# A hybrid decoder step: k, q and scratch laid out by pieces of 128 rows, the third pair's strides reordered, and a longer wait ahead of the out stage

## The reference

```python
DIL_CONFIGS = ((128, 1), (512, 4), (2048, 16))     # window, stride d
def _fold(a, d):                                   # tokens r, r+d, r+2d, ... become one sequence
    n, l, h, dh = a.shape
    return a.reshape(n, l // d, d, h, dh).transpose(0, 2, 1, 3, 4).reshape(n * d, l // d, h, dh)
def _dilated_prompt(q, k, v, slopes):
    for window, d in DIL_CONFIGS:
        o, lse = _band_attention(_fold(q, d)[:, :, :, None], _fold(k, d), _fold(v, d), slopes[:, None], d)
        ...
    return _mix_dilations(outs, lses)              # softmax over the three lse
# _band_attention: blocks of 128 rows; row i reads rows i-128..i, bias -slope*d*distance
```

## Time and profile before

| | |
|---|---|
| median of 3 runs | 1440.73 us (1437.33 to 1441.70) |
| profiled execution | 1441.03 us, span 1439.4 us |
| granted PE clock, mean over the span | 0.976 |
| PE / DVE / ACT / POOL busy | 1347.3 / 714.3 / 461.0 / 215.5 us |
| projection, last matmul | about 788.5 us |
| attention | 792.9 to 1179.4 us |
| first matmul of the out stage | 1192.65 us |

### The profile page before, as it was taken

How to read it: one execution, slowest core, us unless ns; L and a number is a source line. 1 busy time by engine, 2 the same in 40 slices (tenths; PEclk the granted TensorE clock), 3 DMA queues, 4 the chain that set the end, 5 groups by cost and what they waited for, 6 DMA issues and landing times.

```text
span 1439.4 us, 21367 instructions
## 1 busy us (share of the span) xinstructions
PE 1347.3 (94%) x7749; PEld 1167.2 (81%) x7749; DVE 714.3 (50%) x1835; ACT 461.0 (32%) x1189; POOL 215.5 (15%) x264
## 2 busy tenths in 40 slices
PE   5869999999999999999999899999889988999896
PEld 2369999999999999999999676777667647877784
DVE  3592122100335454222121658866789447888783
ACT  5440000121111011222111465666558532343431
POOL 0060000000121211000000053125104310111111
PEclk9989999999999999999999899999999998999998
DMA  8524122121353534444335999945935364555531
GB/s 305 210 87 146 44 87 75 56 87 44 117 184 125 176 103 142 131 140 153 98 117 148 247 261 236 219 105 133 231 87 160 99 208 131 158 177 167 164 125 45
DMA packets 132886, 206.23 MB, mean 143 GB/s; under 512 B 13155, under 2 KB 84484, under 8 KB 130605
## 3 DMA queue, kind: packets, MB, share of 16 engines
q1 hardware_dynamic: 119654, 160.12, 37.7%
q0 software_dynamic: 13152, 45.09, 9.7%
HBM read 136.34 MB, written 68.96 MB: 143 GB/s over the span
## 4 chain that ended last, share of the span: by engine, by line
PE 68%; issue 14%; DVE 7%; DMA 5%; ACT 3%; POOL 2%; SPq 2%; POOLq 0%; DVEq 0%; ACTq 0%
PE psum L973 15%; PE psum L974 15%; PE psum L975 15%; PE psum L1079 4%; PE psum L1106 4%; PE psum L1080 3%; PE psum L1090 3%; PE psum L944 2%; DMA dil_v_p<-kv_nat 2%; PE psum L1115 2%; DMA dec_k<-dil_kc 1%; POOL resid L920 1%; DVE h_f L1470 1%; PE psum L1148 1%; DVE logits L1730 1%
## 5 line engine op out<-in xcount | busy, mean ns | idle before, releaser
L973 PE MATMUL psum<-h_hi,w_hi 128*128 128x416 f32 (+1 forms) x1200 | 422.4, 352 | 12.6 <-POOL h_lo L838 12.6
L974 PE MATMUL psum<-h_lo,w_hi 128*128 128x416 f32 (+1 forms) x1200 | 420.2, 350 | 0.0
L975 PE MATMUL psum<-h_hi,w_lo 128*128 128x416 f32 (+1 forms) x1200 | 419.0, 349 | 0.0
L973 PEld LDWEIGHTS psum<-h_hi,w_hi 128*128 128x128 f32 x1200 | 226.2, 188 | 17.9 <-issue 14.8
L974 PEld LDWEIGHTS psum<-h_lo,w_hi 128*128 128x128 f32 x1200 | 226.2, 189 | 1.4
L975 PEld LDWEIGHTS psum<-h_hi,w_lo 128*128 128x128 f32 x1200 | 226.0, 188 | 1.3
L1352 ACT ACTIVATE probs<-logits,stats 128x256 f32<-128x256 f32 (+1 forms) x352 | 162.2, 462 | 150.2 <-DVE stats L1730 143.9
L1730 DVE CUSTOM_DVE_ANT_0 logits<-psum,bias_dil 128x256 f32<-128x256 f32 (+1 forms) x288 | 93.7, 362 | 83.6 <-PE psum L1080 73.2
L973 PE MATMUL psum<-wo_hi,y_hi 128*128 128x512 f32 x288 | 116.9, 406 | 11.0 <-DVE y_lo L1799 10.8
L975 PE MATMUL psum<-wo_hi,y_lo 128*128 128x512 f32 x288 | 114.3, 397 | 0.0
L974 PE MATMUL psum<-wo_lo,y_hi 128*128 128x512 f32 x288 | 113.9, 396 | 0.0
(11 more groups left out here) (249 smaller groups left out, 1769.0 us busy)
## 6 DMA issues: line engine op xcount, KB each, us to landing
w_raw<-w_tiles POOLq DMA_DIRECT2D x30, 512.0 KB, 6.7
k_both<-qk_dram SPq DMA_DIRECT2D x24, 512.0 KB, 12.5
q_both<-qk_dram SPq DMA_DIRECT2D x40, 256.0 KB, 9.7
mix_dram<-o_st POOLq DMA_DIRECT2D x36, 264.0 KB, 6.0
mix_in<-mix_dram SPq DMA_DIRECT2D x16, 594.0 KB, 4.0
gate_dram<-main SPq DMA_DIRECT2D x9, 1024.0 KB, 3.9
qk_dram<-main_hi SPq DMA_DIRECT2D x9, 1024.0 KB, 4.3
qk_dram<-main_lo SPq DMA_DIRECT2D x9, 1024.0 KB, 7.7
```

What stands on the lines that cost most here:

```text
L973: pe.matmul(out, hi, mhi, start=start, stop=False)
L974: pe.matmul(out, hi, mlo, start=False, stop=False)
L975: return pe.matmul(out, lo, mhi, start=False, stop=stop)
```

## The change

Scratch for keys and queries is split. `q_dram` holds for each piece and head a contiguous stack of high rows and low rows; `k_dram` holds every key row twice (index x). One load of 128 rows now fills both halves of `q_both` or `k_both`, where two loads of 64 rows did it before. In exchange, a key tile is stored by eight transfers of 64 rows (each of the two heads' parts written twice, for high and low), a query tile by four of 64 rows; before, both took two transfers of 128 rows.

Keys stand in the scratch and in `k_both` permuted within each block of 128 tokens: first the 32 tokens with number 0 modulo 4, then those with 1, and so on. Keys of stride 4 are then runs of 32 contiguous columns; keys of stride 16 lie 4 columns apart, and a d16 unit reads its own 128 only. The permutation is made when a key tile leaves PSUM (`key_parts`, 11 pieces a tile on ACT and DVE instead of 5). The bias tables of stride 1 and of the window, and the rows of v for these, follow the same permutation; v rows are loaded by four transfers of 32 rows.

The decode and tail rows' transposes and copies move from ahead of attention into its steps 2 to 14, and the first bias tables move ahead, into the evacuation of the last projection tile. The first window load moves ahead of the decode stores on SP. The third pair's phases become d1, d4, d16. The wait before the out stage's first loads is for all 44 group stores.

```diff
-        qk_dram = scratch("qk_dram", [9, 4, 2, 2, 64, 512])
+        q_dram = scratch("q_dram", [5, 4, 2, 2, 64, 512])
+        k_dram = scratch("k_dram", [4, 4, 2, 2, 2, 64, 512])
...
-            for half in range(2):
-                rows = slice(64 * half, 64 * half + 64)
-                eng.dma_start(q_both[kind][rows, :, cols].bitcast(F32),
-                              qk_dram[qt, j, half].rearrange("h r t -> r h t")).then_inc(done, 16)
-                eng.dma_start(k_both[kind][rows, :, cols].bitcast(F32), k.rearrange("a h r t -> r (a h) t")).then_inc(done, 16)
+            k = k_dram[3, j, p:p + 1] if kind else k_dram[p, j]
+            eng.dma_start(q_both[kind][:, :, cols].bitcast(F32),
+                          q_dram[p + 3 * kind, j].rearrange("h a r t -> (a r) h t")).then_inc(done, 16)
+            eng.dma_start(k_both[kind][:, :, cols].bitcast(F32), k.rearrange("h a x r t -> (x r) (h a) t")).then_inc(done, 16)
+
+        def load_v(eng, dst, v, done):
+
+            for r in range(4):
+                eng.dma_start(dst[32 * r:32 * r + 32], v.rearrange("(b j r) c -> r j b c", j=32, r=4)[r]).then_inc(done, 16)
...
+                t = k_both[self.kind][:, part if self.kind else 2 * h + part, 0:T]
                 if self.d == 16:
-                    r0 = self.r - self.r % 2
-                    return v[:, r0:r0 + 2, :]
-                c0 = P * (self.b - 1) if self.full else 0
-                return v[:, self.r, c0:c0 + 256]
+                    return t.rearrange("p (x s i a) -> p s a x i", x=16, s=4, a=4)[:, self.r % 4, self.r // 4]
+                b0 = self.b - 1 if self.full else 0
+                if self.d == 4:
+                    return t.rearrange("p (x s i) -> p s x i", x=16, s=4)[:, self.r, 4 * b0:4 * b0 + 8]
+                return t[:, P * b0:P * b0 + 256]
...
-                  (0, 2, 0), (0, 2, 2), (0, 2, 1))
+                  (0, 2, 0), (0, 2, 1), (0, 2, 2))
...
+        NEW_STEPS = (5, 7, 9, 11, 13)
...
-                        sp.dma_start(qk_dram[t - K0, :, a].rearrange("j h r t -> (h r) j t"),
-                                     part[b][:, 0:T].bitcast(F32).rearrange("p (j t) -> p j t", j=4)).then_inc(done[b], 16)
+                        for h in range(2):
+                            src = part[b][64 * h:64 * h + 64, 0:T].bitcast(F32).rearrange("r (j t) -> r j t", j=4)
+                            if kind == "q":
+                                dst = (q_dram[t - Q0, :, h, a],)
+                            else:
+                                dst = (k_dram[t - K0, :, h, a, x] for x in range(2))
+                            for d in dst:
+                                sp.dma_start(d.rearrange("j r t -> r j t"), src).then_inc(done[b], 16)
...
-                sp.wait_ge(mix_stored[b], 16 * (20 + (b == 0) + 1))
+                sp.wait_ge(mix_stored[b], 16 * (UNITS // 8 + 1))
...
-                    out = psum[:, S_BANK + n % 2, 256 * h:256 * h + 256]
+                    out = psum[:, S_BANK + n % 2, 256 * h:256 * h + (P if u.d == 16 else 256)]
...
-                    pe.wait_ge(zs_copied, 6)
+                    pe.wait_ge(bank_free[4], NT)
...
+                        for a, z in key_parts(c0, c0 + n):
+                            m = nc.scalar.activation(in_keys(main_hi[b], a, z), in_tokens(bank(g), a - c0, z - c0), ACT.Copy,
+                                                     scale=1.0)
...
+                    if ts == NT - 1 and g == 3:
+                        opening()
```

More of the change, by code:

```diff
@@ L413, in main_stores, with lo_stores @@
         def main_stores(ts):
-            return sum(0 if V0 <= t < K0 else 1 for t in range(ts % 2, ts, 2))
+            return sum(0 if V0 <= t < K0 else 4 if K0 <= t < Q0 else 2 if t >= Q0 else 1 for t in range(ts % 2, ts, 2))
+        def lo_stores(ts):
+            return sum(4 if t < Q0 else 2 for t in range(ts % 2, ts, 2) if t >= K0)
         CHUNK0 = 12
@@ L476, in __init__ @@
                 self.full = self.b > 0
-                self.own = P if self.full or (d == 16 and self.r % 2) else 0
-            def view(self, t):
-                return t[:, 0:T].rearrange("p (t r) -> p r t", r=self.d)
+                self.own = P if self.full else 0
             def spread(self, t):
@@ L1155, in _ @@
                 decode(s - LAST)
+                new_rows(s)
                 if s < UNITS:
@@ L1523, in chunk, with pair_tables, opening @@
                 last.then_inc(yac_ready, 1)
+            def pair_tables(i, kind):
+                off = consts[:, C_OFF:C_OFF + 256]
+                by_key = lambda z: z.rearrange("p (x i s) -> p x s i", x=2, s=4)
+                blocks = lambda z: z.rearrange("p (x s i) -> p x s i", x=2, s=4)
+                for h in range(2):
+                    if kind and h == 0:
+                        dve.wait_ge(lo_stored[1], 16 * lo_stores(NT + 1))
+                    if kind == 0:
+                        slope = consts[:, bass.ds(C_SLD + 2 * i + h, 1)]
+                        for c, d in enumerate(DILATIONS):
+                            src, dst = (by_key(off), blocks(bias_dil[:, c, h, :])) if d == 1 else (off, bias_dil[:, c, h, :])
+                            last = dve.tensor_scalar(dst, src, slope, float(d), ALU.mult, ALU.mult)
+                    else:
+                        slope = consts[:, bass.ds(C_SLS + 2 * i + h, 1)]
+                        last = dve.tensor_scalar(blocks(bias_swa[:, h, :]), by_key(off), slope, None, ALU.mult)
+                if kind:
+                    last = dve.tensor_copy(sink_now[:], neg_sink[:, bass.ds(2 * i, 2)])
+                last.then_inc(bias_ready, 1)
+                dve.wait_ge(bias_ready, 2 * i + kind + 1)
+            def opening():
+                dve.wait_ge(lo_stored[0], 16 * lo_stores(NT))
+                dve.wait_ge(kv_t, len(TURNS))
+                dve.tensor_scalar(neg_sink[:], neg_sink[:], -1.0, None, ALU.mult).then_inc(sink_negated, 1)
+                dve.wait_ge(sink_negated, 1)
+                pair_tables(0, 0)
             def gate_rows():
@@ L1544, in evac @@
                 if ts >= K0 + 2:
[L1545 removed]
+                    dve.wait_ge(lo_stored[b], 16 * lo_stores(ts))
                 if K0 < ts < Q0:
@@ L1721, in _ @@
                     g = s // 4
-                    if u.i == 0 and (u.kind or units[s - 1].kind or s == 0):
+                    if s and u.i == 0 and (u.kind or units[s - 1].kind):
                         pair_tables(u.p, u.kind)
```

115 lines of the change are left out of this document (56 added, 59 removed).

## The result

The changed kernel takes 1443.85 us (median of 20 runs, 1435.85 to 1447.56) against 1440.48 for the kernel before (20 runs): a ratio of 1.0023, 95% interval 1.0013 to 1.0033. It is 0.2% slower: less than the 0.3% that the prediction took for the least difference a measurement can tell, but the interval lies above 1, so it went the other way than the forecast of 1434. The profiled execution took 1443.61 us with a span of 1441.9, 2.5 us more than the span before, so its trace shows the difference well.

What follows compares the result with a forecast made beforehand. PE was taken as the limit, busy 1347 of 1439 us, with waits at attention's start and end. Terms 22 - 8 - 9 - 12 - 8 + 8.5 = -6.5 us gave 1434 us from the 1440.7 median, range 1411 to 1452.

Steps and rivals of the forecast that it cites:

- The copies of decode rows between units go to DVE: Attention's d1 phase: five copies of 0.6 us each hide in its waits, or cost 3 us if those are gone.
- The rest hides: Loads of pairs 1 and 2 run while their phases compute; permuted tables cost the same columns; no time added.
- The stores of keys: Projection's key tiles: 64-row stores at 205 GB/s delay row stores and bank 0, +22 us (0 to +30).
- the sign: Tiles 22 to 25: PE idle 18 to 22 us, ACT waiting for a row store landing 26 us after tile start.
- Rival B: Key stores of 64 rows run near 330 GB/s and no bank waits: 1412 us, chance 0.16.
- The start of attention: Pair 0's first phase: earlier tables, and the last piece's units coming 7 us earlier, give -8 us (-4 to -9).
- The d4 scores: Stride 4 phases of pairs 0 and 1: contiguous key runs make scores as in d1, -9 us together (0 to -13).
- Rival C: The 0.22 us score step comes from `q_ring`, not the keys: about 1463 us, chance 0.05.
- The d16 scores: Stride 16 phases of pairs 0 and 1: 128 keys at 0.12 us a score, -12 us together (0 to -14).
- Rival A: Stride 16 scores stay at 0.22 us: near 1451 us, chance 0.21.
- The third pair: Its last two phases, 87.4 us together: d4 takes about 37 us and d16 with decode work 42.6, -8 us.
- The wait before the out stage: Before the out stage's loads: the last store must land (6.0 us) before the load, +8.5 us (+6 to +11).

Runs made afterwards that it cites:

- E1: Changed kernel with SP's first window load put back behind the decode loads: 1430.28 us, ratio 0.9933 to the kernel before.
- E5: Changed kernel with window load behind the decode loads and second key copies behind the row stores: 1407.97 us, ratio 0.9769 to the kernel before.
- E4: Changed kernel with the second copy of every key row issued behind the tile's four row stores: 1421.70 us, ratio 0.9873 to the kernel before.
- E7: E5 with the first bias tables moved back behind the last evacuation, to DVE's first attention step: 1407.60 us, ratio 0.9776 to the kernel before.
- E9: E3 with the window load behind the decode loads: 1427.76 us, ratio 0.9925 to the kernel before.
- E6: E5 with the third pair's order and the out stage's early wait as before: 1407.72 us, ratio 0.9780 to the kernel before.
- E3: Changed kernel with keys stored twice by four 128-row transfers a tile, each piece loaded by four of 64 rows: 1438.82 us, ratio 0.9994 to the kernel before.

## Why the prediction was wrong

The forecast was -6.5 us and the measurement +3.4, so 10 us are missing. In the trace, the wait at the end of d16 in pair 0 is 10.65 us.

**The step that failed** is in the part on attention's start: "The copies of decode rows between units go to DVE", and behind it "The rest hides". I followed the decode rows on PE and DVE and priced their copies there, but did not follow what they feed: SP's decode stores and loads, moved behind the window load, and POOL, which waits for those loads with the query copies behind it. The same move of the window load was written in the text on the change and has no term in the sum. E1 shows that it is this place in SP's queue: the time falls by 13.6 us against the changed kernel, of which 10.7 are the d16 phase of pair 0. E5 shows that no wait of this size takes its place.

**The stores of keys** were right in place, and in size partly by luck: +22 forecast, +22.5 in the trace. The rate was 204 GB/s at first and 258 later (205 forecast); a weight load of 512 KB, which POOL issued at 603.30, stood among the stores, and ACT waited until 25.5 us after tile 22's start (26 forecast). But two errors cancelled: PE idled for 15.0 us, not the 18 to 22 named as the sign, and the low clock at each stall, 7.5 us over tiles 22 to 25, was not counted. Rival B (no stall) is refuted. That it takes the row stores behind the key stores is shown by E4, where the same transfers in another order cost nothing.

**The start of attention**, -8 forecast and -7.8 found, has the right size for half of a reason. The tables, to which the text gave the first part of the gain, are worth nothing that can be told (E7). The piece loads of 128 rows, which the text gave as the second, carry it: 9 us in d1 of pair 0 (E9 against E5).

**The d4 scores**: -5.0 in pair 1 and -2.1 in pair 0; -9 was forecast for both. In pair 0 the clock was 0.83 behind the wait, but that is not all of it: with the wait gone the phase still took 33.0 us in E1 (clock 0.95) and 34.7 in E5 (0.85), and the cause there stays open. In pair 1 DVE, busy for 27.6 of 31.4 us, is the busiest engine, as said. Rival C, that `q_ring` makes the step, is refuted by the 0.12 us step of d4 with queries from there.

**The d16 scores** cost 0.11 us, 0.12 forecast, and the phase fell by 5.5 us where nothing waited. Rival A is refuted.

**The third pair** gave -9.7, -8 forecast, again with two errors that cancel: d4 took 31.5 us instead of 37 (DVE was busy for 30.0, not 35), and d16 with the decode work 46.2 instead of 42.6. By E5 and E6 some 3 us of the gain are the order's; the rest was there with the old order. **The wait before the out stage** cost 5.8, 8.5 forecast: the last store landed in 3.1 us instead of the 6.0 that the median of that tile gave, a median over the whole kernel, and so also over phases with a DMA share near 1.

So every term that was priced came within 3 us in its sum, d16 of pair 0 without its wait. What failed is a term that was not there.

## What to carry to other kernels

When work is moved, follow it to its last reader through every queue, and list what stands behind the waiting instruction on each: here a load that nobody was in a hurry for, moved forward by a few lines, stopped matmuls two engines further on. Where bytes must be doubled, look at their place in the queue before their number: the same eight transfers cost 22 us when all stand ahead of a store that buffers wait for, and nothing when half of them stand behind it (E4). And price a store's or a load's landing by a row from a stretch with the same traffic, not by the median over the kernel.

## What the runs showed of the hardware

- Key stores of 64 rows moved 204 GB/s in their first 4 us and stores of 128 rows 367 (E3), at a DMA share of 0.98 and 1.03; that is much like the rows of before (205 and 332 GB/s), which were of other transfers. Later in the same tile (611 to 617) stores of 64 rows moved 258, at a share of 1.00.
- A score matmul of 256 columns took 0.22 us at distances of 4 and of 16 columns alike, 0.12 with runs of 32 contiguous columns, and 128 columns at distance 4 took 0.11.
- During each of the three PE waits for bank 0 (4.5 to 6.0 us) and the one at the end of d16 (10.7 us) the granted clock fell to 0.50, its lower level, and stayed there for 6.8 us (three times) and 13.7 us, past the wait's end: tiles 22 to 25 lost 7.5 us to it on top of 15.0 us of idle time.
